# Four reciprocal square roots of a two-block transformer kernel: seven VectorE instructions each, or one power on GpSimd

## The chip, the cores and the metric

The kernel runs on one core of one Trainium2 chip. The metric is the device time in microseconds (us) of one execution. Before the change three executions gave 882.71, 882.89 and 884.42 us; the median is 882.89.

## The reference

Two blocks run one after the other over 256 positions of width 1024. The first block has two layers. Each normalises its input, projects it, runs a Fourier branch, a gated spatial branch and an attention branch with 8 heads, and adds the mix to its input. Queries and keys are normalised per head, over 96 features:

```
def _rmsnorm(t, g):
    tf = t.astype(jnp.float32)
    tf = tf * lax.rsqrt(jnp.mean(tf * tf, axis=-1, keepdims=True) + EPS)
    return (tf * g.astype(jnp.float32)).astype(t.dtype)
...
    q = _rmsnorm(q, q_norm_g)
    k = _rmsnorm(k, k_norm_g)
```

The second block is a mixer followed by a feed-forward stage, each closed by a layer norm:

```
        x = layer_norm(alpha * x + mix, ln1_g[l], ln1_b[l])
        ff = swiglu_ffn(x, w_gate, w_up, w_down)
        x = layer_norm(alpha * x + ff, ln2_g[l], ln2_b[l])
```

`layer_norm` also needs one `rsqrt(var + LN_EPS)` per position. The change is about how these factors, 1/sqrt of a small tile of variances, are computed at four places: for the second layer's query and key heads, for the first layer norm (ln1), and for the two halves of 128 positions of the last layer norm (ln2).

## The kernel before, in words

Every engine has a program of its own, written out by hand in order: `tensor_program`, `scalar_program`, `vector_program`, `gpsimd_program`, `sync_program`. No scheduler reorders them. An engine runs its instructions strictly in that order and waits on semaphores; `V.now()` is the last instruction issued on VectorE, `V[key]`, `M[key]`, `A[key]` are marked points of VectorE, TensorE and ScalarE, `K.pool[key]` of GpSimd. `V.mark(key)` names the present point of VectorE without a new instruction.

Weights come in chunks of 128x1024 (name `raw`), are rounded by ScalarE to `whi` (line 1027) and the remainder is taken by VectorE to `wlo` (`lows`, line 1505); TensorE multiplies high and low parts in up to three passes. TensorE has some 5400 matmuls, and where it would have to wait at a norm it is fed idle matmuls of `modrow` (`keep`, line 524).

`rsqrt(v, u, w)` (lines 1508 to 1518) is the subject: it replaces the tile `v` by 1/sqrt(v) on VectorE. It starts from a guess made on the integer bits (line 1511) and then takes two correction steps of three instructions (lines 1514, 1516, 1518). Each of the seven waits for the one before it.

The four calls that the change touches:

- **Heads of the second layer** (in `layer(1)`, branch `else`). `kv_take`, then three times `hsum` (a sum over 96 features of 16 head rows, line 1772, and one scaling, line 1774) for the first keys, the second keys and the queries. Their variances lie side by side in `stat[:, 144:192]`, 48 columns, so one `rsqrt` serves all. After it come `hscale` (line 1780, 128x1536), `gain` (1791), `fourier` (1706), the rotations `rope` (1800 to 1806), gates, and `heads_T` (1814), which brings transposed keys and queries (transposed by TensorE on line 666) to where the attention scores (line 751) read them.
- **ln1**. TensorE makes the sums (line 961), VectorE the mean (2196), the variance (2199 to 2203), then `rsqrt` on 2 columns, then `diagonal` (2188) puts the factors on a diagonal, TensorE spreads them (966), VectorE scales (2218), ScalarE rounds (1457), and TensorE starts the feed-forward matmuls (431).
- **ln2, twice** (t = 0 and t = 1). The last matmuls of the kernel (line 989) end in PSUM; VectorE adds the residual and sums (2255), makes minus the mean (2257) and the centred rows times the gain (2259) while ScalarE squares (1490); then variance (2261), `rsqrt` on 1 column, and the two final instructions (2266). Each is followed by a DMA to the output; the last one ends the kernel.

GpSimd does almost nothing: twelve additions for the rotary embedding of the second block (line 2277), each behind a wait for VectorE. SyncE issues the DMAs.

Of the kernel before, what the change touches and what calls it, by code (L numbers as in the profile page):

```python
# [10 lines left out]
ALU = mybir.AluOpType  # L11
# [3 lines left out]
P = 128  # L15
# [6 lines left out]
EPS = 1e-6  # L22
LN_EPS = 1e-5
# [1469 lines left out]
def vector_program(K, e):  # L1493
    dv, M, A, V, HI, LO, W, ps, C = Eng(e), K.mm, K.act, K.dve, K.hi, K.lo, K.W, K.ps, K.C
# [13 lines left out]
    def rsqrt(v, u, w):  # L1508

        dv.wait_ge(V.now())  # L1510
        e.tensor_scalar(u.bitcast(I32), v.bitcast(I32), -0.5, 1595932665.0, ALU.mult, ALU.add).then_inc(*V.up())
        for i, (a, c) in enumerate(RSQRT):
            dv.wait_ge(V.now())
            e.tensor_tensor(w, u, u, ALU.mult).then_inc(*V.up())
            dv.wait_ge(V.now())
            e.scalar_tensor_tensor(out=w, in0=w, scalar=a, in1=v, op0=ALU.mult, op1=ALU.mult).then_inc(*V.up())
            dv.wait_ge(V.now())
            e.scalar_tensor_tensor(out=v if i == len(RSQRT) - 1 else u, in0=w, scalar=c, in1=u, op0=ALU.add, op1=ALU.mult).then_inc(*V.up())

    def add_up(src, first, key, *after):  # L1520
        n = src.free_size()
        a = K.acc[:, 0:n]
        dv.wait_ge(V.now(), *after)
        if first:
            e.tensor_copy(a, src).then_inc(*V.up(key))
        else:
            e.tensor_tensor(a, a, src, ALU.add).then_inc(*V.up(key))
# [92 lines left out]
    def layer(l):  # L1620
        g = K.G[l]
# [12 lines left out]
        for m in range(2):  # L1634
            key = (l, "cq", m)
# [3 lines left out]
        key = (l, "ckv", 0)  # L1639
# [44 lines left out]
        def gv_var():  # L1684
            dv.wait_ge(A[l, "gvsq"])
            e.tensor_reduce(va, G2, AX.X, ALU.add).then_inc(*V.up((l, "gvr")))
# [77 lines left out]
        def ss_of(x):  # L1764
            return (g.stat[:, o:o + 16] for o in g.st_of[x])
# [54 lines left out]
        if l == 0:  # L1820
            hsum("k", 0, 0, 0, 0)
            rsqrt(*ss_of(0))
            hscale("k", 0, 0, 0)
            gain("k", 0, 0)
            gv_var()
            gv_factor()
            gv_scale()
            gv_gain()
            hsum("q", 0, 1, 1, 1)
            rsqrt(*ss_of(1))  # L1830
            hscale("q", 0, 1, 1)
            gain("q", 0, 1)
            fourier()
            bias(1, 3)
            for m in range(2):
                dft_parts(m)
            for y in range(2):
                heads_T("k", 0, 0, y, M[l, "dft", 1])
            for y in range(2):
                heads_T("q", 0, 1, y)  # L1840
            for m in range(2):
                dft_gate(m)
            bias(1, 0)
            lows((l, "ukv", 1), 0)
            kv_take(1, 0, M[l, "kT", 0, 1, 4])
            bias(1, 1)
        else:
            kv_take(1, 2)
            gv_var()
            lows((l, "fgate", 1), 0)  # L1850
            hsum("k", 0, 0, 0, 0)
            hsum("k", 1, 2, 2, 2)
            hsum("q", 1, 1, 1, 1)
            rsqrt(g.stat[:, 144:192], g.stat[:, 192:240], g.stat[:, 240:288])
            hscale("k", 0, 0, 0)
            gain("k", 0, 0)
            fourier()
            hscale("q", 1, 1, 1)
            rope("q", 1, 1, 1, 0)
            rope("q", 1, 1, 1, 1)  # L1860
            dft()
            lows((l, "ggate", 0))
            hscale("k", 1, 2, 2)
            gate("ggate", 0, g.ug[:, 0, :])
            lows((l, "gu", 0))
            rope("k", 1, 2, 2, 0)
            rope("k", 1, 2, 2, 1)
            g_u(0)
            gate("ggate", 1, g.ug[:, 1, :])
            for y in range(2):  # L1870
                heads_T("k", 0, 0, y, M[l, "dft", 1])
            heads_T("q", 1, 1, 0)
            for y in range(2):
                heads_T("k", 1, 2, y)
            heads_T("q", 1, 1, 1)
            lows((l, "ggate", 1))
# [104 lines left out]
        for m in range(KD):  # L1981
            key = (l, "wout", m)
# [23 lines left out]
    g = K.G[2]  # L2006
# [178 lines left out]
    v, mu, u, w, m2 = (K.nrm[:, 2 * i:2 * i + 2] for i in range(5))  # L2185
# [16 lines left out]
    dv.wait_ge(M["ln1", "s2"], V.now())  # L2202
    e.scalar_tensor_tensor(out=v, in0=ps.ap(("ln1", "s2"), 2), scalar=1.0 / D, in1=m2, op0=ALU.mult, op1=ALU.subtract).then_inc(*V.up())
    ps.give(("ln1", "s2"), V.now())
    rsqrt(v, u, w)
    diagonal("r", 0, v)
    for k in range(2):
        x1_centre(k)
# [42 lines left out]
    for t in range(2):  # L2251
        nm, v, u, w = (K.nrm[:, 6 * t + i:6 * t + i + 1] for i in (0, 1, 2, 3))
        x, y = g.x3t[:, t, :], g.yt[:, t, :]
        dv.wait_ge(M["fd", KF - 1, t], A["x3t", 2 * t + 1])
        e.tensor_tensor_reduce(x, ps.ap(("fd", t), D), x, 1.0, 0.0, ALU.add, ALU.add, nm).then_inc(*V.up())
        dv.wait_ge(V.now())
        e.tensor_scalar(nm, nm, -1.0 / D, None, ALU.mult, ALU.bypass).then_inc(*V.up(("lnm", t)))
        dv.wait_ge(V.now(), K.l2_in["rows"])
        e.scalar_tensor_tensor(out=y, in0=x, scalar=nm, in1=g.l2g, op0=ALU.add, op1=ALU.mult).then_inc(*V.up())
        dv.wait_ge(A["lnv", t])  # L2260
        e.tensor_scalar(v, v, 1.0 / D, LN_EPS, ALU.mult, ALU.add).then_inc(*V.up())
        rsqrt(v, u, w)
        dv.wait_ge(V.now())
        for q in range(2):
            c = slice(512 * q, 512 * q + 512)
            e.scalar_tensor_tensor(out=y[:, c], in0=y[:, c], scalar=v, in1=g.l2b[:, c], op0=ALU.mult, op1=ALU.add).then_inc(*V.up(("y", t, q)))


def gpsimd_program(K, e):

    gp, V, rot = Eng(e), K.dve, K.G[2].rot
    for gi in range(3):
        for w in range(2):
            for t in range(2):
                a, b = rot[:, t * 1024:t * 1024 + 512], rot[:, t * 1024 + 512:t * 1024 + 1024]
                gp.wait_ge(V["parts", gi, w, t])
                e.tensor_tensor(a, a, b, ALU.add).then_inc(*K.pool.up(("turn", gi, w, t)))


def sync_program(K, e):  # L2280
# [55 lines left out]
def build(nc, cpack, xin, wpack, wmod, l2rows, out):  # L2336
    with ExitStack() as ctx:
# [100 lines left out]
        @block.vector  # L2438
        def _(e):
            vector_program(K, e)  # L2440
# [3 lines left out]
def tables():  # L2444

    f32 = np.float32
    c = {}
    i = np.arange(256)
    a = 2 * np.pi * np.outer(i, i) / 256
    c["c256"] = (np.cos(a) / 128).astype(f32).reshape(2, 128, 256).transpose(1, 0, 2)  # L2450
    c["s256"] = (-np.sin(a) / 128).astype(f32).reshape(2, 128, 256).transpose(1, 0, 2)
    a = 2 * np.pi * np.outer(np.arange(256), np.arange(128)) / 256
    c["cpar"] = (np.cos(a) / 128).astype(f32).reshape(128, 256)
    c["spar"] = (-np.sin(a) / 128).astype(f32).reshape(128, 256)
    j = np.arange(64)
    b = 2 * np.pi * np.outer(j, j) / 64
    for nm, m in (("c64", np.cos(b)), ("s64", np.sin(b))):
        z = np.zeros((128, 128), f32)
        z[:64, :64] = m
        z[64:, 64:] = m  # L2460
        c[nm] = z
    c["ones"] = np.ones((128, 128), f32)
    c["ident"] = np.eye(128, dtype=f32)
    half = 16
    inv = (f32(10000.0) ** (-np.arange(0, half, 2, dtype=f32) / f32(half))).astype(f32)
    row = np.repeat(np.arange(4, dtype=f32), 64)
    col = np.tile(np.arange(64, dtype=f32), 4)
    ar, ac = (row[:, None] * inv[None]).astype(f32), (col[:, None] * inv[None]).astype(f32)
    ang = np.concatenate([ar, ar, ac, ac], -1)
    sgn = np.tile(np.repeat(np.array([-1, 1], f32), 8), 2)  # L2470
    c["cos1"] = np.cos(ang).astype(f32).reshape(2, 128, 32).transpose(1, 0, 2)
    c["sin1"] = (np.sin(ang).astype(f32) * sgn).reshape(2, 128, 32).transpose(1, 0, 2)
    inv2 = (1.0 / (f32(10000.0) ** (np.arange(0, 64, 2, dtype=f32) / f32(64)))).astype(f32)
    ang2 = (np.arange(256, dtype=f32)[:, None] * inv2[None]).astype(f32)
    c["cos2"] = np.cos(ang2).astype(f32).reshape(2, 128, 32).transpose(1, 0, 2)
    c["sin2"] = np.sin(ang2).astype(f32).reshape(2, 128, 32).transpose(1, 0, 2)
    c["nsin2"] = -c["sin2"]
    t, s = np.arange(256)[:, None], np.arange(256)[None, :]
    m = []
    for win, dil in ((128, 1), (512, 4), (2048, 16)):  # L2480
        ok = (t >= s) & ((t - s) % dil == 0) & ((t - s) <= win)
        m.append(np.where(ok, 0.0, NEG).astype(f32))
    c["mask1"] = np.stack([x[128:, :] for x in m], 1)
    e = np.zeros((128, 4), f32)
    e[:, 0], e[:, 1] = EPS, LN_EPS
    c["eps"] = e
    z = np.zeros((128, 2), f32)
    z[0, 0] = z[1, 1] = z[2, 0] = z[3, 1] = 1.0
    c["sel"] = z
    return c  # L2490
# [75 lines left out]
```

## Time and profile before

| | before |
|---|---|
| time, median of 3 | 882.89 us |
| the profiled execution | 882.33 us, of it span 880.4 us |
| TensorE matmul busy | 860.0 us (98% of the span) |
| VectorE busy | 640.5 us (73%), 1273 instructions |
| ScalarE busy | 448.1 us (51%) |
| GpSimd busy | 21.2 us (2%), 16 instructions |
| chain that ended last | TensorE 68%, VectorE 25%, ScalarE 3%, DMA 2% |

The span is what the profiler sees from the first to the last instruction; the time is longer by 1.9 us that lie around it. "Busy" of TensorE includes the overlap of pipelined matmuls. The chain that ended last is followed back from the last instruction of the kernel, at each step to what released it.

### The profile page before, as it was taken

The numbers are of one execution on the slowest core, as the hardware profiler recorded it, in microseconds if no ns is written. First come the engines' busy times: TensorE is split into PE (matmuls) and PEld (weight loads), VectorE is DVE, ScalarE is ACT, GpSimd is POOL, SyncE is SP. The second block draws the span as 40 slices with busy tenths as digits, with TensorE's granted clock in tenths as the row PEclk, the third lists the DMA queues.
The fourth block names the chain that finished last, engine by engine and source line by source line (L and its number), as shares of the span: only waits on it lengthen the run. The fifth ranks groups of instructions, "written<-read, shape, count | busy, mean of one in ns | idle before, by whom it ended". The sixth has DMA issues, their size and how long they took to land.

```text
span 880.4 us, 13502 instructions
## 1 busy us (share of the span) xinstructions
PE 860.0 (98%) x5412; PEld 713.4 (81%) x5412; DVE 640.5 (73%) x1273; ACT 448.1 (51%) x761; POOL 21.2 (2%) x16
## 2 busy tenths in 40 slices
PE   8999999999999999999999999999999999999996
PEld 5678678777686888778998888989999888888885
DVE  5535869675656789966699999977598866565566
ACT  3353445554633564755444444556554765555552
POOL 0000000000000000000003113000000000000000
PEclk9999999999999999999999999999999999999999
DMA  9785543202173134213655665532466365655641
GB/s 357 298 308 189 214 186 113 84 1 82 39 263 104 41 102 166 86 42 113 207 193 168 194 199 178 151 119 68 120 192 222 113 208 179 213 172 187 207 152 49
DMA packets 40719, 138.28 MB, mean 157 GB/s; under 512 B 4432, under 2 KB 4560, under 8 KB 40400
## 3 DMA queue, kind: packets, MB, share of 16 engines
q1 hardware_dynamic: 40224, 134.41, 45.4%
q10 hardware_dynamic: 432, 3.00, 0.9%
q8 instruction: 43, 0.70, 0.3%
q14 instruction: 20, 0.16, 0.1%
HBM read 136.34 MB, written 1.05 MB: 156 GB/s over the span
## 4 chain that ended last, share of the span: by engine, by line
PE 68%; DVE 25%; ACT 3%; DMA 2%; issue 1%; SPq 0%; DVEq 0%; ACTq 0%
PE ps L415 8%; DVE wlo L1505 7%; PE ps L989 6%; DVE AF L2023 6%; PE ps L416 4%; PE ps L370 4%; PE ps L371 4%; PE ps L375 3%; PE ps L751 3%; PE ps L489 3%; PE ps L387 2%; PE ps L398 2%; DMA AF<-wmod 2%; PE ps L774 2%; PE ps L399 2%; PE ps L402 2%
## 5 line engine op out<-in xcount | busy, mean ns | idle before, releaser
L1027 ACT ACTIVATE whi<-raw 128x1024 fp32r<-128x1024 f32 (+3 forms) x213 | 211.3, 1001 | 100.4 <-DMA raw<-wpack 54.5
L1505 DVE TENSOR_TENSOR wlo<-raw,whi 128x1024 fp32r<-128x1024 f32 (+3 forms) x213 | 240.9, 1154 | 28.6 <-ACT whi L1027 28.4
L370 PE MATMUL ps<-hx,whi 128*128 128x256 f32 (+1 forms) x384 | 115.7, 301 | 0.5 <-ACT AF L1383 0.3
L415 PE MATMUL ps<-hx,whi 128*128 128x512 f32 x320 | 113.9, 399 | 0.0
L371 PE MATMUL ps<-hx,whi 128*128 128x256 f32 (+1 forms) x384 | 112.1, 292 | 0.0
L375 PE MATMUL ps<-hx,wlo 128*128 128x256 f32 (+1 forms) x332 | 97.1, 292 | 0.0
L416 PE MATMUL ps<-hx,wlo 128*128 128x256 f32 x320 | 90.0, 281 | 0.0
L370 PEld LDWEIGHTS ps<-hx,whi 128*128 128x128 f32 x384 | 73.5, 191 | 4.1 <-issue 2.3
L371 PEld LDWEIGHTS ps<-hx,whi 128*128 128x128 f32 x384 | 73.6, 192 | 2.0 <-issue 0.7
L415 PEld LDWEIGHTS ps<-hx,whi 128*128 128x128 f32 x320 | 60.2, 188 | 14.4
L460 PE MATMUL ps<-whi,hx 128*128 128x512 f32 (+1 forms) x192 | 71.1, 370 | 0.5 <-DVE lat L1641 0.5
L462 PE MATMUL ps<-whi,hx 128*128 128x512 f32 (+1 forms) x192 | 70.3, 366 | 0.0
L461 PE MATMUL ps<-wlo,hx 128*128 128x512 f32 (+1 forms) x192 | 70.3, 366 | 0.0
L375 PEld LDWEIGHTS ps<-hx,wlo 128*128 128x128 f32 x332 | 63.5, 191 | 1.1
L416 PEld LDWEIGHTS ps<-hx,wlo 128*128 128x128 f32 x320 | 60.6, 189 | 0.7
L2023 DVE SCALAR_TENSOR_TENSOR AF<-AF,cst 128x256 f32<-128x256 f32 x120 | 58.0, 529 | 0.4
L989 PE MATMUL ps<-whi,hx 128*128 128x512 f32 x176 | 50.6, 392 | 0.0
L1899 DVE TENSOR_REDUCE AF<-ps 128x1 f32<-128x512 f32 (+1 forms) x48 | 28.7, 598 | 28.2 <-PE ps L751 28.1
L1265 ACT ACTIVATE AF<-ps,AF 128x512 f32<-128x512 f32 (+1 forms) x48 | 29.5, 615 | 29.7 <-DVE AF L1899 29.2
L1272 ACT ACTIVATE AF<-ps 128x512 f32<-128x512 f32 (+1 forms) x48 | 24.9, 522 | 38.1 <-PE ps L759 38.1
L751 PE MATMUL ps<-AF 96*128 96x512 f32 (+1 forms) x96 | 43.1, 530 | 0.7 <-DVE AF L1814 0.7
L2242 DVE TENSOR_TENSOR AF<-AF,ps 128x256 f32<-128x256 f32 x20 | 8.4, 422 | 46.1 <-ACT AF L1477 46.1
(309 smaller groups left out, 1711.7 us busy)
## 6 DMA issues: line engine op xcount, KB each, us to landing
raw<-wpack SPq DMA_DIRECT2D x181, 512.0 KB, 4.3
AF<-wmod SPq DMA_DIRECT2D x48, 512.0 KB, 6.8
raw<-wpack SPq DMA_DIRECT2D x24, 256.0 KB, 3.2
raw<-wpack SPq DMA_DIRECT2D x6, 384.0 KB, 3.0
XT<-xin SPq DMA_DIRECT2D x4, 512.0 KB, 5.6
raw<-wpack SPq DMA_DIRECT2D x4, 432.0 KB, 4.9
cst<-cpack ACTq DMA_DIRECT2D x1, 1349.0 KB, 9.2
AF<-l2rows ACTq DMA_DIRECT2D x1, 1024.0 KB, 5.9
```

The lines of the kernel that those rows point to most:

```text
L370: e.matmul(o, wh[:, b], xh(k), start=j == 0, stop=False, skip_group_check=True)
L371: e.matmul(o, wh[:, b], xl(k), start=False, stop=False, skip_group_check=True)
L375: e.matmul(o, wl[:, b], xh(k), start=False, stop=False, skip_group_check=True)
L415: e.matmul(ps.ap(key, 512).rearrange("p (s n) -> p s n", s=2), wh[:, b], K.hx[:, :, k, 0:256], start=k == 0, stop=False, skip_group_check= ...
L416: i = e.matmul(ps.ap(key, 256), wl[:, b], hh[:, k, 0:256], start=False, stop=k == KD - 1, skip_group_check=True)
L460: e.matmul(o, xh(k)[:, ts], wh[:, b], start=k == 0, stop=False, skip_group_check=True)
L461: e.matmul(o, xh(k)[:, ts], wl[:, b], start=False, stop=False, skip_group_check=True)
L462: i = e.matmul(o, xl(k)[:, ts], wh[:, b], start=False, stop=k == KD - 1, skip_group_check=True)
L989: i = e.matmul(ps.ap(("fd", t), 512, 512 * q), y[:, f % 8, x], w[:, 512 * q:512 * q + 512], start=f == 0 and y is K.fh and w is wh, stop=f ...
L1027: e.activation(W.hi(i), W.raw(i), ACT.Copy).then_inc(*HI.up(j))
L1505: e.tensor_tensor(W.lo(i), W.raw(i), W.hi(i), ALU.subtract).then_inc(*LO.up(j))
L2023: e.scalar_tensor_tensor(out=g.CV[:, m, :], in0=g.U[:, m, j:j + 256], scalar=w, in1=g.CV[:, m, :], op0=ALU.mult, op1=ALU.add).then_inc(*V. ...
```

## The change

Four calls of `rsqrt` in the vector program become `pool_rsqrt`: VectorE marks where the variance is ready and waits for GpSimd. GpSimd raises the tile, in place, to the power -0.5, with one instruction on two tensors; the exponent is a new constant in a free column of a table that is loaded anyway. The other calls of `rsqrt` stay on VectorE. No DMA is added or moved, and the order of the instructions that remain is as before on every engine.

```
+    def pool_rsqrt(key):
+
+        V.mark(("var", key))
+        dv.wait_ge(K.pool["rsqrt", key])
...
-            rsqrt(g.stat[:, 144:192], g.stat[:, 192:240], g.stat[:, 240:288])
+            pool_rsqrt("heads")
...
-    rsqrt(v, u, w)
+    pool_rsqrt("ln1")
...
-        rsqrt(v, u, w)
+        pool_rsqrt(("ln2", t))
...
+    def rsqrt(key, v):
+        gp.wait_ge(V["var", key])
+        e.tensor_tensor(v, v, C("eps", 2, 1).broadcast_to([P, v.free_size()]), ALU.pow).then_inc(*K.pool.up(("rsqrt", key)))
+
+    rsqrt("heads", K.G[1].stat[:, 144:192])
     for gi in range(3):
...
+    rsqrt("ln1", K.nrm[:, 0:2])
+    for t in range(2):
+        rsqrt(("ln2", t), K.nrm[:, 6 * t + 1:6 * t + 2])
...
-    e[:, 0], e[:, 1] = EPS, LN_EPS
+    e[:, 0], e[:, 1], e[:, 2] = EPS, LN_EPS, -0.5
```

VectorE's program at the second layer's heads, before: the last head sum and its scaling, the seven instructions on the 48 variances, and the scaling of the first keys (`AF` is the big tile in which all of this lies).

```order
L1772 TENSOR_REDUCE AF<-AF 128x16
L1774 TENSOR_SCALAR AF<-AF 128x16
L1511 TENSOR_SCALAR AF<-AF 128x48
L1514 TENSOR_TENSOR AF<-AF 128x48
L1516 SCALAR_TENSOR_TENSOR AF<-AF 128x48
L1518 SCALAR_TENSOR_TENSOR AF<-AF 128x48
L1514 TENSOR_TENSOR AF<-AF 128x48
L1516 SCALAR_TENSOR_TENSOR AF<-AF 128x48
L1518 SCALAR_TENSOR_TENSOR AF<-AF 128x48
L1780 TENSOR_TENSOR AF<-AF 128x1536
L1791 TENSOR_TENSOR AF<-AF,cst 128x16x32
```

The same place now. The line numbers are five higher.

```order
L1777 TENSOR_REDUCE AF<-AF 128x16
L1779 TENSOR_SCALAR AF<-AF 128x16
L1785 TENSOR_TENSOR AF<-AF 128x1536
L1796 TENSOR_TENSOR AF<-AF,cst 128x16x32
L1711 COPY AF<-ps 128x512 x2
L1505 TENSOR_TENSOR wlo<-raw,whi 128x1024
```

Seven rows are gone, and the scaling that followed them now stands behind the wait for GpSimd. It is the same at the last norm. Before, VectorE's last rows, for t = 1 (`nrm` is the small tile of means and variances):

```order
L2261 TENSOR_SCALAR nrm<-nrm 128x1
L1511 TENSOR_SCALAR nrm<-nrm 128x1
L1514 TENSOR_TENSOR nrm<-nrm 128x1
L1516 SCALAR_TENSOR_TENSOR nrm<-nrm 128x1
L1518 SCALAR_TENSOR_TENSOR nrm<-nrm 128x1
L1514 TENSOR_TENSOR nrm<-nrm 128x1
L1516 SCALAR_TENSOR_TENSOR nrm<-nrm 128x1
L1518 SCALAR_TENSOR_TENSOR nrm<-nrm 128x1
L2266 SCALAR_TENSOR_TENSOR AF<-AF,nrm 128x512 x2
```

And GpSimd's program now, where line 2280 is the power and line 2288 the twelve additions that were there before:

```order
L2280 TENSOR_TENSOR AF<-AF,cst 128x48
L2288 TENSOR_TENSOR AF<-AF 128x512 x12
L2280 TENSOR_TENSOR nrm<-nrm,cst 128x2
L2280 TENSOR_TENSOR nrm<-nrm,cst 128x1 x2
```

The power on 48 columns is GpSimd's first work after its start-up; the other three follow the additions.

## Rows read from the trace of the kernel before

**Rows 1.** The page: busy time of each engine, share, instructions.

```profile
PE 860.0 (98%) x5412; PEld 713.4 (81%) x5412; DVE 640.5 (73%) x1273; ACT 448.1 (51%) x761; POOL 21.2 (2%) x16
```

**Rows 2.** Chain of waits, last 20 us: start, us, engine and line.

```profile
861.21 5.48 PE ps L989 x24
...
869.46 0.15 DVE nrm L2261
...
869.63 0.16 DVE nrm L1511
...
870.99 1.42 DVE AF L2266 x2
...
875.06 0.15 DVE nrm L2261
...
875.23 0.17 DVE nrm L1511
...
876.59 0.75 DVE AF L2266
```

**Rows 3.** Timeline from 871 us: start, us, engine, line, tiles.

```profile
871.50 0.61 PE L989 MATMUL ps<-whi,hx 128*128 128x512 f32 x2
...
872.32 1.22 DVE L2255 CUSTOM_DVE_ANT_0 AF<-ps,AF 128x1024 f32<-128x1024 f32 x1
```

**Rows 4.** Chain of waits at ln1, 680 to 686 us.

```profile
681.60 0.17 DVE nrm L2203
681.79 0.18 DVE nrm L1511
...
683.17 0.44 DVE wk L2188
683.65 0.71 PE ps L966 x2
684.39 0.49 DVE wk L2218
684.91 0.52 ACT hx L1457
```

**Rows 5.** Timeline of TensorE at ln1, with its idle time in brackets.

```profile
683.65 0.70 PE L966 MATMUL ps<-wk,cst 128*128 128x256 f32 x2 [0.79 <-DVE wk L2188]
```

**Rows 6.** Chain of waits at the second layer's heads, 332 to 358 us.

```profile
332.59 0.19 DVE AF L1774
332.80 0.20 DVE AF L1511
...
334.48 1.77 DVE AF L1780
...
354.56 3.30 DVE AF L1814 x5
```

**Rows 7.** Timeline of TensorE where the attention of the second layer begins.

```profile
356.19 1.04 PE L666 MATMUL ps<-cst,wk 128*96 128x128 f32 x8
357.90 0.70 PE L751 MATMUL ps<-AF 96*128 96x512 f32 x1 [0.68 <-DVE AF L1814]
```

**Rows 8.** Timeline of GpSimd: its start-up, and the first and third addition.

```profile
0.24 0.10 POOL L2500 MEMSET const-float32-0.0<- 128x1 f32 x1 [0.24 <-issue]
...
465.31 1.29 POOL L2277 TENSOR_TENSOR AF<-AF 128x512 f32<-128x512 f32 x1 [464.87 <-DVE AF L2045]
...
477.69 1.30 POOL L2277 TENSOR_TENSOR AF<-AF 128x512 f32<-128x512 f32 x1 [8.79 <-DVE AF L2045]
```

**Rows 9.** Timeline of VectorE: what releases those two additions.

```profile
464.81 0.42 DVE L2045 TENSOR_TENSOR AF<-ps,cst 128x256 f32<-128x256 f32 x1
...
477.19 0.42 DVE L2045 TENSOR_TENSOR AF<-ps,cst 128x256 f32<-128x256 f32 x1
```

**Rows 10.** Timeline of the last norm: handing over from VectorE to ScalarE and back.

```profile
873.58 0.15 DVE L2257 TENSOR_SCALAR nrm<-nrm 128x1 f32<-128x1 f32 x1
873.77 1.15 ACT L1490 ACTIVATE AF<-AF,nrm 128x1024 f32<-128x1024 f32 x1 [4.36 <-DVE nrm L2257]
...
874.83 0.19 ACT L1490 ACTIVATION_READ_ACCUMULATOR AF<-AF,nrm 128x1 f32 x1
875.04 0.15 DVE L2261 TENSOR_SCALAR nrm<-nrm 128x1 f32<-128x1 f32 x1
```

**Rows 11.** Groups of ScalarE: loading of a table, count, sum, mean ns.

```profile
L1048 ACT ACT_TABLE_LOAD x1 | 1.3, 1283 | 1.5 <-DVE AF L1579 1.5
```

**Rows 12.** Stretch table at ln1: busy by engine, granted clock, DMA share.

```profile
680.00:684.00 4.00, 3.21 (x22) 2.68 (x22) 3.29 (x16) 0.26 (x1) 0.00 (x0) 1.00 0.96 344
```

More of the change, by code:

```diff
@@ L2269, in gpsimd_program @@
 def gpsimd_program(K, e):
-    gp, V, rot = Eng(e), K.dve, K.G[2].rot
+    gp, V, C, rot = Eng(e), K.dve, K.C, K.G[2].rot
+    def rsqrt(key, v):
+        gp.wait_ge(V["var", key])
+        e.tensor_tensor(v, v, C("eps", 2, 1).broadcast_to([P, v.free_size()]), ALU.pow).then_inc(*K.pool.up(("rsqrt", key)))
+    rsqrt("heads", K.G[1].stat[:, 144:192])
     for gi in range(3):
```

## The prediction

> **What bounds the kernel now.** I read the page's busy times first [rows 1]: TensorE is busy 98% of the span, GpSimd 2%. So a shorter VectorE program is worth nothing by itself; a saving counts only where TensorE waits for VectorE, or where VectorE works after TensorE's end. The chain of waits then tells whether the four places are of that kind.
>
> At the end of the kernel they are. TensorE's matmuls for the first half end at 866.69 (861.21 + 5.48) [rows 2], and from there the chain is VectorE almost alone, through the seven instructions of t = 0 and those of t = 1, up to the last output DMA. At ln1 the chain runs through the seven as well, then line 2188, TensorE's spreading, VectorE, ScalarE and the first feed-forward matmuls [rows 4], and TensorE sits idle for 0.79 us behind this chain even though it has been fed idle matmuls [rows 5]. At the heads of the second layer the chain is on VectorE from the head sums to line 1814 without a pause worth naming [rows 6], and TensorE waits for it once, 0.68 us, before the first attention scores [rows 7]; until then its own work covers it.
>
> **What the seven cost at each place.** I take the distance from the end of the instruction before them to the start of the one behind them, from the chain.
>
> - ln2, t = 1: 875.06 + 0.15 = 875.21 to 876.59, 1.38 us [rows 2].
> - ln2, t = 0: 869.46 + 0.15 = 869.61 to 870.99, 1.38 us [rows 2].
> - ln1: 681.60 + 0.17 = 681.77 to 683.17, 1.40 us [rows 4].
> - heads: 332.59 + 0.19 = 332.78 to 334.48, 1.70 us [rows 6].
>
> **What takes their place.** A hand-over to GpSimd, the power, a hand-over back. The first is in the trace: VectorE's line 2045 ends at 465.23 and 477.61 [rows 9], and GpSimd starts at 465.31 and 477.69 [rows 8], 0.08 us each time. The way back from GpSimd to VectorE isn't in the trace; from VectorE to ScalarE it is 0.04 us (873.73 to 873.77), from ScalarE to VectorE 0.02 (875.02 to 875.04) [rows 10]. I take 0.05, with 0.02 and 0.08 as bounds. Together 0.13 us. So each place gains 1.25 (both ln2), 1.27 (ln1) and 1.57 us (heads) less the power's own duration; call the latter p.
>
> **The power's duration** is the unknown that decides. No row has a power, and none has a GpSimd instruction on two small tensors. From below: a GpSimd memset of one column takes 0.10 us [rows 8], and the addition over 512 columns 1.29, so (1.29 - 0.10)/512 = 2.3 ns a column; a power at an addition's rate would take 0.10 us on one or two columns and 0.10 + 48 x 0.0023 = 0.21 us on 48. From above: on one or two columns the whole 512-column addition, 1.29 us; on 48 columns, a memset's whole 0.10 us for every one of them, 4.8 + 0.1 = 4.9 us. Between such ends I go by ratios rather than halves for the wide one (square root of 0.21 x 4.9 = 1.0), and move up a little, because a power has many steps where an addition has one: 1.2 us. For one or two columns the ratio mean is 0.36 and the plain mean 0.70; I take 0.5 between them.
>
> The Trainium skill has a rule against this change, "GPSIMD Engine Reference", § 4.1 Engine selection: elementwise work belongs on VectorE, since GpSimd is about twice as slow on two inputs. The rule compares one instruction with one, and here one replaces seven dependent ones. By it a power would take twice a VectorE step of about 0.2 us, 0.4 us at all four places, and the gains would be 0.68, 0.87, 0.19 and 0.85, in all 2.6 us. No row here shows whether a power is priced like other elementwise work.
>
> **Part by part.**
>
> - Heads: VectorE reaches line 1780 earlier by 1.57 - 1.2 = 0.37 us, and everything behind it moves along. TensorE's wait of 0.68 us shrinks by 0.37. This place can never give more than that 0.68, as TensorE's own transposes end at 357.23 [rows 7]. A loss, in contrast, would be passed on whole once it is behind the heads: queued behind the waiting instruction are the copies of the Fourier branch that free PSUM (1706), low weight parts (1505), rotations and transposed heads, and TensorE waits for all of them. Gain 0.37; bounds 0.68 and -3.3.
> - ln1: 1.27 - 0.5 = 0.77 us, all of it, since there the chain has no parallel branch: behind the wait stand 2188 and the centring of two tiles (2193), and TensorE has only idle matmuls to run. The granted clock is 1.00, the 2.4 GHz level, through this stretch with the pause in it [rows 12], so a shorter pause changes nothing of it. Gain 0.77; bounds 1.17 and -0.02.
> - ln2, t = 0: the end of TensorE's last matmul sets a floor. It ends at 872.11, and VectorE starts line 2255 for t = 1 at 872.32 [rows 3]. With 0.02 us for the release, the first half can give 0.19 us at most. The rest, 0.75 - 0.19 us, only makes VectorE wait for TensorE. Gain 0.19; bounds 0.19 and -0.04.
> - ln2, t = 1: 1.25 - 0.5 = 0.75 us straight off the end; only the two final instructions and the output DMA follow. Gain 0.75; bounds 1.15 and -0.04.
>
> No DMA is moved, and GpSimd's twelve additions are 130 us away from either neighbour, so their start isn't touched. The start-up of GpSimd and the constant cost nothing that ends late: the exponent lies in a table loaded at the start.
>
> Sum: 0.37 + 0.77 + 0.19 + 0.75 = 2.08 us. Against the profiled execution: 882.33 - 2.08 = 880.25. That execution is 0.56 us quicker than the median of the three timed ones, so on the median the forecast is 882.89 - 2.08 = 880.8 us. What a measurement of this kernel can tell from no change is about 0.2%, 1.77 us; "faster" begins below 881.12.
>
> **Rivals.**
>
> 1. *The power costs about as much as the seven.* At p = 1.0 on one or two columns and 1.6 on 48, the terms are -0.03, 0.27, 0.19, 0.25, in all 0.7 us: 882.2. For it: GpSimd's only real work in the trace is slow, 1.29 us for what is an ordinary addition. Against it: nearly all of that is the 512 columns, and the memset shows a small fixed part.
> 2. *Slower: the power is priced by the column, and the wide one at the heads pays for it.* One mechanism, at one place. With a fixed 0.5 us and a memset's 0.10 for each column p is 0.5 + 4.8 = 5.3 at the heads, 0.5 to 0.7 elsewhere. The heads lose 5.3 - 1.57 = 3.7 us, and the others keep 0.57 + 0.19 + 0.65 = 1.4 to 1.7 us. About 2.1 us slower: 885.0. The heads lose at all from p = 1.57 on; the whole change loses when that term exceeds 1.7, at p = 3.3, or (3.3 - 0.5)/48 = 58 ns a column, 25 times an addition's. For it: VectorE's seven steps hardly grow with the columns (1.38 us for 1, 1.70 for 48), so VectorE is at its best there, and a power is a long calculation. Against it: an addition's 2.3 ns.
> 3. *A high fixed price for every power.* With 2.0 us on small tiles and 2.5 on 48 the terms are -0.93, -0.73, -0.75, -0.75, so 3.2 us slower: 886.1. It decides from p = 1.25 on. Against it: the memset's 0.10 and the 0.08 us of hand-over.
> 4. *The first instruction of its kind loads its code.* The power at the heads is GpSimd's first real work. In rows, the first addition after 464.87 us of idleness starts 0.08 us after its release and takes 1.29 us, the third 1.30 [rows 8], so no load is seen. The nearest thing that has one is ScalarE's table load, 1.28 us [rows 11]; that much at the heads would leave 1.57 - 1.2 - 1.28 = -0.91 there and 0.8 us in all: 882.1. The Trainium skill, "GPSIMD Engine Reference", § 2.1 Instruction dispatch, says that the first call to a freshly loaded kernel pays about 6 us that no instruction in the profile shows. By that price the heads would lose 5.6 us and the kernel would take 886.8. The trace disagrees for the addition, and no run here shows it for a power.
>
> **How the numbers follow.** The forecast, a power well under the seven, has a chance of 0.50 and lies below 881.12 in 0.48. Rival 1 has 0.26, rival 2 0.14, rival 3 0.05, rival 4 0.05. Within 0.2% lie rival 1, rival 4, a small form of rival 2 and the forecast's rest: 0.26 + 0.05 + 0.01 + 0.02 = 0.34. Slower by over 0.2% are the rest of rival 2 and rival 3: 0.13 + 0.05 = 0.18. Lower end of the range: the lower bounds of the power give 0.68 + 1.17 + 0.19 + 1.15 = 3.2 us, 879.7; less 0.3 for the spread of runs (the two lower ones are 0.2 apart), 879.4. Upper end: up to rival 2, 885.0. The forecast's own range is 879.4 to 881.6.
>
> **What the profile after would show.** Three powers of about 0.5 us and one of about 1.2 on GpSimd; VectorE's line behind each starts 0.13 us more than that after the variance; at ln1 TensorE's 0.79 us of idleness nearly gone; at the attention's start its 0.68 us cut to some 0.3; VectorE waiting for TensorE before line 2255 of t = 1; 28 fewer VectorE instructions. I am wrong if a power takes over 1.25 us on one column or over 1.6 on 48, if the way back takes much over 0.1 us, or if a longer pause of VectorE at the heads sets other waits behind it that the chain doesn't show now.

## The result and the profile after

The kernel became slower by half a per cent. Six executions each gave 888.34 us in the median after (887.31 to 888.98) and 883.76 us before (882.71 to 885.51); the ratio is 1.0050 with a 95% interval of 1.0037 to 1.0063, so 3.3 to 5.6 us. The forecast was 880.8 us and its range ended at 885.0. The kernel before was itself 0.87 us slower in these six executions than in the three that the forecast started from (882.89 us). One execution of the kernel before, made beside experiment seven, took 1422.46 us at a granted clock of 0.556 and is left out of that experiment's ratio.

The page's busy times, in the order of [rows 1]:

```profile
PE 862.3 (97%) x5412; PEld 714.4 (81%) x5412; DVE 635.6 (72%) x1245; ACT 448.6 (51%) x761; POOL 31.0 (4%) x20
```

VectorE lost 28 instructions and 4.9 us of work, GpSimd gained four and 9.8 us. That 9.8 for four small instructions is the first sign. GpSimd's timeline shows them; columns are start, duration, line, tiles, count and, in brackets, the idle time before and what ended it:

```profile
333.67 8.02 POOL L2280 TENSOR_TENSOR AF<-AF,cst 128x48 f32<-128x48 f32 x1 [333.23 <-DVE AF L1779]
...
689.08 0.72 POOL L2280 TENSOR_TENSOR nrm<-nrm,cst 128x2 f32<-128x2 f32 x1 [133.51 <-DVE nrm L2208]
876.34 0.55 POOL L2280 TENSOR_TENSOR nrm<-nrm,cst 128x1 f32<-128x1 f32 x1 [186.53 <-DVE nrm L2266]
881.77 0.56 POOL L2280 TENSOR_TENSOR nrm<-nrm,cst 128x1 f32<-128x1 f32 x1 [4.89 <-DVE nrm L2266]
```

One column 0.55 us, two 0.72, and 48 columns 8.02. The narrow ones are as forecast (0.5); the wide one was put at 1.2, and at 4.9 in the worst case.

The chain of waits at the heads, to be held against [rows 6]:

```profile
331.63 1.76 DVE AF L1777
333.39 0.02 issue
333.42 0.19 DVE AF L1779
333.60 0.07 issue
333.67 8.03 POOL AF L2280
341.70 0.02 issue
341.73 1.77 DVE AF L1785
```

From the end of line 1779 to the start of 1785 it is now 341.73 - 333.60 = 8.13 us, where it was 1.70. The hand-overs are small, as forecast: 0.07 us there and 0.02 back. TensorE's timeline shows what that did:

```profile
344.87 1.17 PE L709 MATMUL ps<-cst,AF 128*128 128x256 f32 x2 [4.73 <-DVE AF L1711]
...
365.13 1.13 PE L751 MATMUL ps<-AF 96*128 96x512 f32 x2 [0.68 <-DVE AF L1819]
```

The first wait is new. TensorE has no use for the heads' factors on line 709; it waits for the copies of the Fourier branch (1711), which VectorE issues behind the wait for GpSimd. The second is the wait of 0.68 us of [rows 7], unchanged in length, 7.23 us later. After the pause the granted clock fell. The stretch table (length, busy time and instructions of TensorE, of its weight loads, VectorE, ScalarE and GpSimd, then the clock, DMA share and GB/s):

```profile
338.00:342.00 4.00, 2.13 (x18) 1.93 (x17) 0.27 (x1) 1.36 (x3) 3.69 (x1) 1.00 0.00 0
342.00:346.00 4.00, 1.14 (x3) 0.96 (x4) 3.97 (x5) 0.00 (x0) 0.00 (x0) 0.87 0.00 0
346.00:350.00 4.00, 4.00 (x16) 3.29 (x14) 3.90 (x9) 0.00 (x0) 0.00 (x0) 0.71 0.44 131
350.00:354.00 4.00, 4.00 (x34) 3.93 (x33) 3.97 (x11) 1.44 (x2) 0.00 (x0) 1.00 0.08 7
```

The clock goes from the 2.4 GHz level (1.00) partly to 1.2 GHz (means of 0.87 and 0.71) and back. Here it costs nothing: TensorE is still 0.68 us ahead of VectorE at line 751.

At ln1 and at the end the change did what it was meant to. The chain at ln1, against [rows 4]:

```profile
688.85 0.17 DVE nrm L2208
689.01 0.07 issue
689.08 0.73 POOL nrm L2280
689.81 0.02 issue
689.83 0.44 DVE wk L2193
690.27 0.04 issue
690.31 0.71 PE ps L966 x2
```

689.01 to 689.83 is 0.82 us, for 1.40 before. TensorE's idle time of [rows 5] went from 0.79 to 0.21 us. VectorE's timeline of the last norm, against [rows 2, 3]:

```profile
876.10 0.15 DVE L2266 TENSOR_SCALAR nrm<-nrm 128x1 f32<-128x1 f32 x1
876.92 1.41 DVE L2271 SCALAR_TENSOR_TENSOR AF<-AF,nrm 128x512 f32<-128x512 f32 x2 [0.67 <-POOL nrm L2280]
878.81 1.23 DVE L2260 CUSTOM_DVE_ANT_0 AF<-ps,AF 128x1024 f32<-128x1024 f32 x1 [0.48 <-PE ps L989]
...
881.54 0.15 DVE L2266 TENSOR_SCALAR nrm<-nrm 128x1 f32<-128x1 f32 x1
882.37 1.42 DVE L2271 SCALAR_TENSOR_TENSOR AF<-AF,nrm 128x512 f32<-128x512 f32 x2 [0.67 <-POOL nrm L2280]
```

0.67 us in place of 1.38 both times, and the half-way wait for TensorE (0.48 us) that caps what t = 0 can give.

The whole difference of the two spans, from the starts of the same lines in both traces:

| stretch | before | after | difference |
|---|---|---|---|
| start of the program to the third head sum (1772, 1777) | 330.81 | 331.63 | +0.82 |
| to the first scores (751) | 27.09 | 33.50 | +6.41 |
| to the second spreading of ln1 (966) | 325.75 | 325.18 | -0.57 |
| to the first sum of ln2 (2255, 2260) | 183.06 | 183.06 | 0.00 |
| to the sum of t = 1 | 5.61 | 5.44 | -0.17 |
| to its final instruction (2266, 2271) | 4.27 | 3.56 | -0.71 |
| sum | | | +5.78 |

The spans are 886.2 and 880.4. The first line is not put down to the change: none of the changed instructions runs ahead of that point, and over the nine profiled executions of this case the third head sum starts anywhere between 330.27 and 332.36 us. Without it the traces give +4.96 us, inside the timed 3.3 to 5.6.

### The profile page after: what moved, and what is told of

Read it like the earlier page. It is cut to its first block, busy times and chain, and to the rows that moved or that the text cites. A ratio compares the mean times of both kernels' runs of the same rounds, so it can differ in the third digit from the quotient of the medians.

```text
span 886.2 us, 13482 instructions
## 1 busy us (share of the span) xinstructions
PE 862.3 (97%) x5412; PEld 714.4 (81%) x5412; DVE 635.6 (72%) x1245; ACT 448.6 (51%) x761; POOL 31.0 (4%) x20
## 4 chain that ended last, share of the span: by engine, by line
PE 67%; DVE 24%; ACT 4%; DMA 2%; issue 2%; POOL 1%; SPq 0%; DVEq 0%; POOLq 0%; ACTq 0%
PE ps L415 8%; DVE wlo L1505 7%; PE ps L989 6%; DVE AF L2028 6%; PE ps L416 4%; PE ps L370 4%; PE ps L371 4%; PE ps L375 3%; PE ps L751 3%; PE ps L489 3%; DMA AF<-wmod 2%; PE ps L398 2%; PE ps L387 2%; PE ps L774 2%; PE ps L399 2%; PE ps L402 2%
```

## The experiments

Each ratio is against executions of the kernel before that were made beside the experiment. Their median was 883.36 us for experiments one to four, 882.97 for five and six, and 884.5 for seven, so a ratio says more than a difference of two medians from different experiments.

**One: the heads back on VectorE.** `pool_rsqrt("heads")` and GpSimd's first power are undone; ln1 and ln2 stay changed.

```
-            pool_rsqrt("heads")
+            rsqrt(g.stat[:, 144:192], g.stat[:, 192:240], g.stat[:, 240:288])
...
-    rsqrt("heads", K.G[1].stat[:, 144:192])
```

> The changed kernel with the heads' factors back on VectorE (seven instructions on 48 columns); ln1 and both ln2 stay powers on GpSimd. Theory A (a power costs about 0.39 us plus 0.16 us for each column, and only the wide one loses): the span is shorter than the kernel before's by 0.58 us at ln1, 0.2 at ln2 t = 0 and 0.71 at ln2 t = 1, together 1.5 us; VectorE goes from the last head scaling to its line 1780 work in 1.7 us again, and TensorE has no wait of 4.7 us in the layer. Rival B (any use of GpSimd for these factors sets the rest back, for example by the 0.8 us by which the changed kernel was already late at 333 us): no faster than before, 0 to 1 us slower.

Measured: 882.19 us, ratio 0.9980 (0.9969 to 0.9991), 0.8 to 2.7 us faster than before. From the third head sum to the first scores it is 27.10 us (27.09 before). The two spreadings of ln1 stand 1.74 us apart, for 2.33. So the narrow powers gain by themselves, and Rival B falls. The trace shows 1.14 us less than before from the third head sum to the end, not the 1.5 of Theory A: between the first scores and ln1, where nothing was changed, this execution took 0.35 us more (323.77 for 323.42).

**Two: only the heads on GpSimd.** The complement: ln1 and ln2 get their `rsqrt` on VectorE back.

```
-    pool_rsqrt("ln1")
+    rsqrt(v, u, w)
...
-        pool_rsqrt(("ln2", t))
+        rsqrt(v, u, w)
```

> Only the heads' factors are a power on GpSimd (128x48); ln1 and ln2 are as before. Theory A: the power takes 8.0 us, VectorE waits 8.1 us where it took 1.7 before, and nearly all of the difference, 6.4 us, arrives at the end: about 6.4 us over the kernel before. Rival B (part of the delay is absorbed in attention, and the remainder of the 4.6 us came from elsewhere): 3 to 5 us over.

Measured: 889.62 us, ratio 1.0066 (1.0048 to 1.0085), 4.2 to 7.5 us slower. From the third head sum (330.93) to the first scores (364.44) it is 33.51 us, 6.42 more than before, and from there to the first spreading of ln1 323.45 us, for 323.42 before. Attention absorbs nothing of it, and by the trace Rival B falls.

**Three: the price of a power by itself.** All four places on VectorE; behind the twelve additions GpSimd, otherwise idle, runs a row of instructions on a free area of SBUF:

```
+    def price(op, n, parts=P):
+        x = bx[0:parts, 0:n]
+        gp.wait_ge(K.pool.now())
+        e.tensor_tensor(x, x, C("eps", 2, 1, parts).broadcast_to([parts, n]), op).then_inc(*K.pool.up())
```

> The kernel before, and on GpSimd behind its twelve additions a row of instructions on two tensors on a scratch area, each waiting for the one before: power on 128 partitions x 48, 48, 1, 2, 4, 8, 16, 32, 96 columns; product and sum on 1, 48 and 96; power on 64, 32, 16 and 1 partitions x 48; power of 1.0 on 48. Theory A (a loop over columns that costs the same for every column): 8.0, 8.0, 0.55, 0.7, 1.0, 1.7, 2.9, 5.5 and 15.7 us; product and sum 0.15 to 0.4 us; 16 to 64 partitions the same 8.0 us. Rival D (the first power loads its code): the first of the two powers on 48 columns takes 8.0 us, the second about 2 us or less. Rival E (element by element): the power on one partition takes about a sixteenth, 0.5 to 1 us. The two don't exclude Theory A's slope for whole columns. The time of the kernel isn't the point; it should be that of the kernel before, since GpSimd is idle there.

Measured, from GpSimd's timeline, some of the twenty:

```profile
548.22 8.23 POOL L2294 TENSOR_TENSOR modrow<-modrow,cst 128x48 f32<-128x48 f32 x1
556.53 8.30 POOL L2294 TENSOR_TENSOR modrow<-modrow,cst 128x48 f32<-128x48 f32 x1
564.91 0.58 POOL L2294 TENSOR_TENSOR modrow<-modrow,cst 128x1 f32<-128x1 f32 x1
566.35 1.01 POOL L2294 TENSOR_TENSOR modrow<-modrow,cst 128x4 f32<-128x4 f32 x1
567.44 1.69 POOL L2294 TENSOR_TENSOR modrow<-modrow,cst 128x8 f32<-128x8 f32 x1
572.79 5.42 POOL L2294 TENSOR_TENSOR modrow<-modrow,cst 128x32 f32<-128x32 f32 x1
578.28 15.70 POOL L2294 TENSOR_TENSOR modrow<-modrow,cst 128x96 f32<-128x96 f32 x1
594.07 0.99 POOL L2294 TENSOR_TENSOR modrow<-modrow,cst 128x1 f32<-128x1 f32 x1
595.48 0.35 POOL L2294 TENSOR_TENSOR modrow<-modrow,cst 128x96 f32<-128x96 f32 x1
595.91 0.19 POOL L2294 TENSOR_TENSOR modrow<-modrow,cst 128x1 f32<-128x1 f32 x1
597.19 7.99 POOL L2294 TENSOR_TENSOR modrow<-modrow,cst 64x48 f32<-64x48 f32 x1
621.39 7.99 POOL L2294 TENSOR_TENSOR modrow<-modrow,cst 1x48 f32<-1x48 f32 x1
629.70 8.00 POOL L2294 TENSOR_TENSOR modrow<-modrow,cst 128x48 f32<-128x48 f32 x1
```

The first eight-odd microseconds are paid again by the second power on 48 columns, so they are not the loading of code (Rival D falls). From 1 to 96 columns the durations lie within 0.06 us of 0.39 us plus 0.159 us a column (48 columns by the last five powers, 7.99 and 8.00 us; the row on 16 columns apart). One partition costs as much as 128 (Rival E falls): the duration goes by the columns and not by the partitions. The value didn't matter between those tried: powers of 1.0 (the last row) take 8.00 us, and the kernel's own variances took 8.02. A product on 96 columns (the row at 595.48) takes 0.35 us, so the price is the power's own, not that of two tensors on GpSimd. The kernel's time, one execution, was 881.81 us, about that of the kernel before, as expected.

Some rows are off. The first two powers on 48 columns took 0.2 to 0.3 us more than the later ones, and the power on 16 columns 3.50 us for 2.94; the next experiment has 2.91 for two of its three and 3.35 for the third. VectorE was at work beside the quick ones too, and which of its instructions hold a power up wasn't tried. Furthest off is the first product, on one column: 0.99 us (the row at 594.07), where a sum on one column takes 0.19 (595.91) and the expectation said 0.15 to 0.4. VectorE had a large product of two tensors running just then:

```profile
593.78 1.22 DVE L1505 TENSOR_TENSOR wlo<-raw,whi 128x1024 fp32r<-128x1024 f32 x1
```

It ends at about 595.0, and GpSimd's product at 595.06. That fits a GpSimd instruction held up by VectorE; a cost of the first product of its kind would look the same, and the two weren't tried apart.

**Four: three narrow powers in place of the wide one, each begun early.** The heads' variances don't become ready together: the first keys' are there 4.6 us ahead of the queries'. Here each goes to GpSimd as soon as its own sum is scaled, and VectorE waits for each just ahead of the scaling that uses it.

```
             hsum("k", 0, 0, 0, 0)
+            V.mark(("var", "k0"))
             hsum("k", 1, 2, 2, 2)
+            V.mark(("var", "k1"))
             hsum("q", 1, 1, 1, 1)
-            pool_rsqrt("heads")
+            V.mark(("var", "q1"))
+            dv.wait_ge(K.pool["rsqrt", "k0"])
...
+            dv.wait_ge(K.pool["rsqrt", "q1"])
             hscale("q", 1, 1, 1)
...
+            dv.wait_ge(K.pool["rsqrt", "k1"])
             hscale("k", 1, 2, 2)
...
-    rsqrt("heads", K.G[1].stat[:, 144:192])
+    for key, o in (("k0", 144), ("k1", 176), ("q1", 160)):
+        rsqrt(key, K.G[1].stat[:, o:o + 16])
```

> The changed kernel with the heads' power in three of 16 columns, each started as soon as its own sum is scaled (first keys, second keys, queries), and VectorE waits for each only before the scaling that uses it. Theory A: each takes 0.39 + 16 x 0.159 = 2.9 us. The first runs from 328.3 to 331.2 beside VectorE's other sums, the second to 334.2, the third to 337.1, all before they are needed (332.8, 347.9, 339.2), so VectorE waits for none and gains 1.6 us there; TensorE's wait of 0.68 us before the attention scores goes. With the norms: 0.68 + 0.58 + 0.2 + 0.71 = 2.2 us faster than the kernel before. Rival C (GpSimd working beside VectorE slows VectorE's sums and products at the memory they share, as an addition took 2.2 instead of 1.3 us beside VectorE): VectorE's instructions between 328 and 338 us grow by over 10% and the gain at the heads is nil; 1.5 us faster or less.

Measured: 880.37 us, ratio 0.9966 (0.9953 to 0.9979), 1.9 to 4.2 us faster than before. This version is faster than both kernels, by 0.3% against the one before. The timing alone doesn't separate it from experiment one (0.9969 to 0.9991), so what the three pieces add is read from the traces. GpSimd's timeline:

```profile
328.76 2.91 POOL L2285 TENSOR_TENSOR AF<-AF,cst 128x16 f32<-128x16 f32 x1 [328.32 <-DVE AF L1779]
331.64 2.91 POOL L2285 TENSOR_TENSOR AF<-AF,cst 128x16 f32<-128x16 f32 x1
334.52 3.35 POOL L2285 TENSOR_TENSOR AF<-AF,cst 128x16 f32<-128x16 f32 x1
```

VectorE's, at the first scaling, then what stands before the queries' scaling:

```profile
333.08 0.18 DVE L1779 TENSOR_SCALAR AF<-AF 128x16 f32<-128x16 f32 x1
333.36 1.76 DVE L1785 TENSOR_TENSOR AF<-AF 128x1536 f32<-128x1536 f32 x1
...
336.97 0.69 DVE L1711 COPY AF<-ps 128x512 f32<-128x512 f32 x1 [0.52 <-PE ps L697]
```

VectorE waits for no power: 1785 starts 0.1 us after 1779's end, the third power ends at 337.87 and is wanted at 338.71. VectorE's own instructions are as long as before (sums 1.75, scalings 1.76 us), so Rival C falls for powers. For additions the trace of the kernel before shows the opposite: six of the 120 instructions of VectorE's line 2023 take 1.51 or 1.52 us where the median is 0.48, each of them started while one of GpSimd's additions of 2.2 us was running. One such pair, GpSimd's row first:

```profile
479.15 2.20 POOL L2277 TENSOR_TENSOR AF<-AF 128x512 f32<-128x512 f32 x1 [0.16 <-DVE AF L2045]
480.11 1.52 DVE L2023 SCALAR_TENSOR_TENSOR AF<-AF,cst 128x256 f32<-128x256 f32 x1
```

From the third head sum to the first scores it is 26.10 us, 0.99 less than before. VectorE saves 1.6 us at first, gives 0.52 of it back waiting for TensorE's line 697, and TensorE's wait before the scores, 0.68 before, is still 0.28:

```profile
357.39 1.12 PE L751 MATMUL ps<-AF 96*128 96x512 f32 x2 [0.28 <-DVE AF L1819]
```

**Five: the three pieces without the norms.** ln1 and ln2 on VectorE, as in experiment two.

> Only the heads' factors on GpSimd, as three powers of 16 columns, each started behind its own sum; ln1 and ln2 as in the kernel before. Theory A: VectorE waits for none of them, the stretch from the third head sum to the first attention scores is 1.0 us shorter than before, and so is the kernel. Rival H (the gain seen in the trace with the norms changed too is given back in attention or later): no change beyond 0.3 us.

Measured: 882.78 us, ratio 0.9996 (0.9984 to 1.0007): from 1.4 us faster to 0.6 slower. The trace again has 26.10 us at the heads and 323.43 from there to ln1 (323.42 before), so in this execution 0.99 us are gained at the heads and not given back before ln1. The timing can't confirm a gain of that size, nor does it exclude Rival H, which stays open.

**Six: the Fourier copies ahead of the wait.** The 48-column power as in the changed kernel, but VectorE's next work that doesn't need it comes first.

```
-            pool_rsqrt("heads")
-            hscale("k", 0, 0, 0)
-            gain("k", 0, 0)
+            V.mark(("var", "heads"))
             fourier()
+            dv.wait_ge(K.pool["rsqrt", "heads"])
+            hscale("k", 0, 0, 0)
+            gain("k", 0, 0)
```

> The changed kernel, with the copies of the Fourier branch (line 1711, two of 128x512) and the low weight part behind them moved ahead of VectorE's wait for the 48-column power; the power itself is as in the changed kernel. Theory A (the 8 us reach the end because VectorE runs in order: what stands behind the wait is late, whether it needs the factors or not): the copies start at about 337 us instead of 344, TensorE's wait of 4.7 us before its line 709 goes, and what was moved, 1.2 + 1.1 = 2.4 us of VectorE's work, now lies inside the wait, so the attention scores start about 2.4 us sooner than in the changed kernel: some 2.4 us faster than it, 2.5 us slower than the kernel before. Rival F (the loss goes by TensorE's wait of 4.7 us alone): the loss of the heads falls to 6.4 - 4.7 = 1.7 us or less, and the kernel is within 1 us of the one before. Rival G (it goes by the factors alone): no change against the changed kernel.

Measured: 887.23 us, ratio 1.0052 (1.0034 to 1.0070), so 3.0 to 6.2 us slower than before, which doesn't separate it from the changed kernel. In the trace the stretch at the heads is 31.88 us: 1.62 less than with the change, not the 2.4 of Theory A. VectorE's wait for the power is 2.59 us instead of 8.13, and TensorE's wait at 709 is gone. But TensorE now runs into the next wait, for low weight parts that stand behind the power all the same (4.3 us), and the clock falls right before its densest part. The row of that wait, then the stretches around it:

```profile
351.50 0.42 PE L370 MATMUL ps<-hx,whi 128*128 128x256 f32 x1 [4.33 <-DVE wlo L1505]
...
346.00:350.00 4.00, 1.18 (x10) 0.97 (x9) 3.86 (x15) 0.38 (x1) 0.00 (x0) 1.00 0.00 0
350.00:354.00 4.00, 2.50 (x12) 2.50 (x13) 4.00 (x5) 0.00 (x0) 0.00 (x0) 0.72 0.38 124
354.00:358.00 4.00, 4.00 (x31) 4.00 (x30) 3.97 (x9) 1.70 (x2) 0.00 (x0) 0.86 0.83 268
```

TensorE doesn't wait for VectorE ahead of line 751 any more. So it has become the late one, and part of VectorE's gain is gone there. That the lower clock is what made it late fits these rows, but wasn't tried apart. Rival F falls: of the 6.41 us lost at the heads 4.79 are still lost, not 1.7. Rival G falls by the trace alone, since the timing doesn't separate this kernel from the changed one. So the loss isn't one wait, and it isn't the factors alone: what stands behind the wait in VectorE's queue counts.

**Seven: a fourth place, 4 columns.** As experiment four, and the factors of the norm ahead of the second layer on GpSimd too.

```
-        rsqrt(v, u, w)
+        if key == ("h", 1):
+            pool_rsqrt("h1")
+        else:
+            rsqrt(v, u, w)
```

> The kernel with the heads' power in three pieces, and with one more place on GpSimd: the factors of the norm ahead of the second layer, 4 columns, where VectorE takes from 281.43 to 282.86 = 1.43 us for the seven instructions. Theory A (0.39 us + 0.16 us for each column, 0.08 us to GpSimd and 0.03 us back): a power of 1.03 us, 1.14 us in all, so the stretch is 0.29 us shorter than before, and all four norms and heads together put the kernel some 2.7 us below the kernel before. Rival I (the rule fits only the sizes it was made from, or GpSimd's first power pays more than a later one): the stretch is not shorter, and the kernel is as the one with three pieces or slower.

Measured: 881.41 us, ratio 0.9966 (0.9953 to 0.9979), the same ratio as experiment four, so the further gain that was forecast, 0.3 us or more, is neither shown nor excluded by the timing. GpSimd's first power takes what the rule says:

```profile
283.06 1.02 POOL L2288 TENSOR_TENSOR nrm<-nrm,cst 128x4 f32<-128x4 f32 x1 [282.62 <-DVE nrm L1551]
```

and VectorE's stretch is 1.13 us, 0.30 shorter, as expected. In the trace it brings nothing: TensorE runs 16 matmuls of the modulation in its queue ahead of the spreading, and starts the latter when they are done, 2.43 us after their start, for 2.44 before:

```profile
282.71 2.50 PE L489 MATMUL ps<-AF 128*32 128x512 f32 x16
285.14 1.12 PE L518 MATMUL ps<-wk,cst 128*128 128x512 f32 x2
```

From VectorE's variance (282.82) to TensorE's first matmul of the layer (287.87) it is 5.05 us, against 5.07. The rule of the price held; the forecast of a further gain didn't, because here VectorE's seven instructions were not what TensorE waited for.

## Why the prediction was wrong

- **What bounds the kernel**: right. At all four places the chain ran through the seven instructions, and every difference of more than 0.2 us behind the start lies at one of them.
- **What the seven cost and what handing over costs**: right. 1.38, 1.38, 1.40 and 1.70 us were replaced, and the hand-overs were 0.09 us together, where 0.13 was taken.
- **The power's duration on one or two columns**: right, 0.55 and 0.72 for 0.5.
- **The power's duration on 48 columns**: this is the step that failed. The prediction took 1.2 us, by the ratio mean between an addition's rate and a memset for every column, and called 4.9 us the bound from above. It is 8.02. No row bounded a power's price per column; a memset's 0.10 us was a number of the right unit, not a bound. 0.159 us a column is 1.6 times that, and 68 times an addition's 2.3 ns. Experiment three measures it, and one and two show that it is this term alone: without the wide power the kernel is faster, with it alone 4.2 to 7.5 us slower (6.4 in the trace).
- **Heads**: forecast gain 0.37, measured loss 6.41. With the measured duration the prediction's own sum gives 1.57 - 8.02 = -6.45, and its statement that a loss is passed on whole was right. The forecast cap of 0.68 us was too low: when no power is waited for, 0.99 is gained (experiments four and five). The cap took the end of TensorE's transposes (357.23) as fixed, but they move along with VectorE: counted from the third head sum they end 26.42 us on before and 25.81 in experiment four.
- **ln1, ln2**: 0.77, 0.19 and 0.75 were forecast; 0.57, 0.17 and 0.71 came. ln1 is less mainly because the second column costs its 0.16.
- **The rivals**: rival 2 was the right mechanism at the right place, with a chance of 0.14, and its size was that of the same wrong bound: 0.10 us a column gave 885.0. By its own threshold of 58 ns a column the whole change loses, and 159 ns is far past it. Rival 1 (about as much as the seven) holds for no place. Rival 3 (a high fixed price) falls by 0.39 us. Rival 4 falls by experiments three and seven: the second power on 48 columns is as long as the first, and the first power of a kernel takes 1.02 us on 4 columns. The 6 us that the Trainium skill, "GPSIMD Engine Reference", § 2.1 Instruction dispatch, gives for a first call to a freshly loaded kernel show in none of these rows, and not as idle time ahead of one either: GpSimd starts the power of experiment seven 0.08 us after VectorE's variance is done (282.98 to 283.06).
- The rule weighed in the prediction, GpSimd about twice as slow as VectorE on two inputs (the Trainium skill, "GPSIMD Engine Reference", § 4.1 Engine selection), would have put 48 columns at 0.4 us. For a power the trace disagrees by a factor of twenty; the measurement decides. For ordinary work it is about right: GpSimd's addition on 512 columns takes 1.29 us [rows 8], and VectorE's product on 512 columns (line 1791) 0.69.

The range was wrong in the main for one reason. Its upper end was built on a bound that no row supported, while the term it bounded was the only one able to move the kernel by more than 3 us. The 0.87 us by which the kernel before was slower this time is the smaller part: without it the result would still lie over 885.0.

## What to carry to other kernels

A power on GpSimd costs 0.39 us plus 0.16 us for each column here, however few partitions it has, and 0.1 us for handing over both ways; VectorE's seven dependent instructions cost 1.4 us on one column and 1.7 on 48. So, as an estimate from these rows, it pays up to about five columns if VectorE has to wait for it (1.28 us against 1.4; one, two and four columns were run), and on more only where its result isn't wanted yet: cut the wide one, start each piece when its own input is ready, and wait just before the use. The traces of experiments four, five and seven show 0.99 us for that at the heads, a gain too small for the timing of experiment five to confirm. And a shorter stretch on VectorE is worth something only where TensorE waits for it or has ended, as experiment seven shows. An instruction kind with no row in the trace deserves a price measurement before it is put on the path, and a range that doesn't end at the nearest other instruction.

## What was not expected of the hardware

- One partition and 128 partitions cost a power the same 8.0 us on 48 columns.
- A 16-column power took 2.91 us twice, and 3.35 and 3.50 us in two other places; powers on 48 columns took 8.0 to 8.3.
- Beside a power VectorE's instructions took as long as without one, while six of its instructions took 1.52 us in place of 0.48 beside an addition on GpSimd.
- After TensorE's pause of 4.7 us the granted clock was 0.87 and 0.71 in the next two stretches of 4 us and 1.00 again in the third. It cost nothing where VectorE was still the later of the two.
